# A router taken apart by row tile, fixed room for every expert in DRAM, and the experts' low parts on one engine

## The chip, the cores and the metric

The kernel runs on one core of a Trainium2 chip. The metric is the time of one execution on the device, in microseconds (us). Three timed runs of the kernel before gave 829.58, 831.20 and 831.58 us; their median, 831.2 us, is the time before.

## What is computed

One layer of a gated trunk over 512 rows of width 1024, all in float32:

```
xn = rms_norm(x, norm1_g)
x  = x + hybrid_mixer(xn, ...)        # attention, spatial gating and recurrence; gated, merged, then @ w_out
xn = rms_norm(x, norm2_g)
g_logits = xn @ wg + bg               # 4 groups
e_logits = xn @ we + be               # 16 experts, 4 in a group
# the best group; in it the two best experts by softmax; their two weights are normalised, times the group's probability
for e in range(16):
    h = silu(xn @ w_gate[e]) * (xn @ w_up[e])        # 1024 -> 512
    y = y + combine[:, e] * (h @ w_down[e])          # 512 -> 1024
return rms_norm(x + y, final_norm_g)
```

Each row goes to two of 16 experts, so each expert has 64 rows on average. The kernel brings an expert's rows together in a tile of 128 rows; an expert with more than 128 rows gets further tiles.

## The kernel before

**Products.** Every weight is split in two, `w_hi` (rounded to the format of the matrix engine) by ScalarE (`split_hi`, L354, and `split_hi_loop`, L361) and the rest `w_lo` by a subtraction (`split_lo`, L366, and `split_lo_loop`, L372). A product is three matmuls (`three`, L988 to L990). Weights come in blocks of 128x1024, from a ring of four buffers before the experts and 24 (EVEN and ODD, 12 each) in them; `w_hi` and `w_lo` have four places each. Before the experts GpSimd makes the low parts. In the experts `on_pool(r)` is true for the first four blocks of the first tile alone; VectorE makes the low parts of all others.

**Stages.** First come the projections of `x` (8 blocks), four pairs of heads and channels (5 blocks each), the gates with the branch products (36 blocks), and the output projection: 4 blocks for columns 0 to 511 (PSUM banks 4 to 7), then 4 for columns 512 to 1023, this half by row tile `t` (banks 0 to 3). Between the loads of one pair and the next SyncE queues a quarter of the stores that fill `slots`, the DRAM room for the experts' rows, with zeros (L452): 24 tiles of 512 KB in all.

**Router.** For each row tile of the second half: VectorE adds `x` (L1610), ScalarE squares (L882), GpSimd takes the power -1/2 (L607), VectorE makes `xn2` (L1616), TensorE turns it (`turn_xn2`, L1185), ScalarE copies it (L889), TensorE multiplies by the router's weights (`logits`, L1176). With the logits of all 512 rows VectorE picks group and experts (L1655 to L1680), TensorE counts the rows ahead of each row at its expert (L1217, L1220), and VectorE makes the one-hot matrix of tile 0 in `silu` (L1689), the place of every row in `slots` (L1695 to L1717), the table of tiles (L1719 to L1729) and the weights (L1733 to L1742). TensorE gathers tile 0 by 64 matmuls with `silu` (L1251); ScalarE and VectorE split it in `xT_hi` and `xT_lo` (L901, L1747). GpSimd scatters `xn2` to `slots` by eight indirect DMAs (L618); the other tiles are read back from there.

**Experts.** Tile `i` uses 12 blocks: gate and up of tile `i` and down of the tile before, so the program's `tile(i)` ends with the result of expert `i-1`, which ScalarE copies (`y_part`, L920) and stores to `slots` over its own rows (L922). Tiles 1 to 13 are unrolled in pairs, those from 14 on are in a loop whose count and experts are loaded to registers from `tile_table`. Here there are 16 tiles. Room `k` of `slots` is expert `k`'s for its first 128 rows; rooms from 16 on are for what is over. At the end GpSimd gathers for each row its first expert's result (L645) once all tiles but the last are stored (`before_last_stored`), and its second when the last is stored (`all_stored`); VectorE adds them (L1804, L1823) and normalises (L1811, L1816).

**Order.** Each engine's program is written out by hand and runs in order, with semaphores between engines. VectorE's `link` makes the next instruction wait for the one it wraps. SyncE issues all loads; its loads of tile 2 from the fourth block on wait for the scatter.

## Time and profile before

| | |
|---|---|
| median of three runs | 831.2 us |
| the profiled execution's own time | 831.56 us |
| span, first to last instruction | 829.8 us |
| TensorE busy, mean granted clock | 773.4 us (93%), 0.969 |
| VectorE, ScalarE, GpSimd busy | 486.0, 448.5, 213.8 us |
| chain that ended last | PE 80%, DVE 8%, ACT 6%, issue 2%, DMA 2%, POOL 1% |

```profile
PE   6999999999999999999999957999999999999950
DVE  6603657576633223023122275788989898998955
POOL 3654333232323444444425143000000000000013
PEclk9999999999999999999999959999999999999995
```

Each digit is a fortieth of the span, 20.7 us: the engine's busy share in tenths and, in the last row, TensorE's granted clock in tenths of full speed. The matmul engine is full but for the start, slices 24 and 25 (the router) and the end.

### The profile page before, as it was taken

The numbers are of one execution on the slowest core, as the hardware profiler recorded it, in microseconds if no ns is written. First come the engines' busy times: TensorE is split into PE (matmuls) and PEld (weight loads), VectorE is DVE, ScalarE is ACT, GpSimd is POOL, SyncE is SP. The second block draws the span as 40 slices with busy tenths as digits, with TensorE's granted clock in tenths as the row PEclk, the third lists the DMA queues.
The fourth block names the chain that finished last, engine by engine and source line by source line (L and its number), as shares of the span: only waits on it lengthen the run. The fifth ranks groups of instructions, "written<-read, shape, count | busy, mean of one in ns | idle before, by whom it ended". The sixth has DMA issues, their size and how long they took to land.

```text
span 829.8 us, 10565 instructions
## 1 busy us (share of the span) xinstructions
PE 773.4 (93%) x3639; PEld 635.7 (77%) x3639; DVE 486.0 (59%) x640; ACT 448.5 (54%) x572; POOL 213.8 (26%) x126
## 2 busy tenths in 40 slices
PE   6999999999999999999999957999999999999950
PEld 4887888888788888888888856887888888787840
DVE  6603657576633223023122275788989898998955
ACT  6245565565642323223222306688887888887832
POOL 3654333232323444444425143000000000000013
PEclk9999999999999999999999959999999999999995
DMA  8664561612122443323357349999999999957945
GB/s 300 183 243 162 179 227 53 228 53 76 51 77 70 148 138 102 102 89 89 101 176 285 109 182 350 399 398 403 388 409 397 410 407 402 401 226 274 334 152 203
DMA packets 126490, 186.24 MB, mean 224 GB/s; under 512 B 9133, under 2 KB 61941, under 8 KB 126454
## 3 DMA queue, kind: packets, MB, share of 16 engines
q1 hardware_dynamic: 119156, 167.82, 56.3%
q10 hardware_dynamic: 4994, 9.56, 3.0%
q0 software_dynamic: 2304, 8.39, 2.8%
q8 instruction: 22, 0.36, 0.2%
q14 instruction: 14, 0.11, 0.0%
HBM read 158.47 MB, written 27.28 MB: 224 GB/s over the span
## 4 chain that ended last, share of the span: by engine, by line
PE 80%; DVE 8%; ACT 6%; issue 2%; DMA 2%; POOL 1%; ACTq 1%; DVEq 0%; SPq 0%
PE ps L988 24%; PE ps L990 23%; PE ps L989 23%; PE ps L1228 2%; DVE w_lo L372 1%; PE ps L1251 1%; PE ps L1066 1%; PE ps L1092 1%; PE ps L1176 1%; ACT w_hi L361 1%; PE ps L1235 1%; DMA x<-in_x 1%; DMA slots<-y_tile 1%; DMA raw_mg<-slots,slot_idx 1%; PE ps L1077 1%
## 5 line engine op out<-in xcount | busy, mean ns | idle before, releaser
L366 POOL TENSOR_TENSOR w_lo<-raw,w_hi 128x1024 fp32r<-128x1024 f32 x72 | 174.0, 2419 | 256.5 <-ACT w_hi L354 256.5
L354 ACT ACTIVATE w_hi<-raw 128x1024 fp32r<-128x1024 f32 x73 | 77.0, 1058 | 182.5 <-PE ps L990 174.7
L988 PE MATMUL ps<-xn_hi,w_hi 128*128 128x512 f32 x352 | 141.8, 403 | 0.0
L990 PE MATMUL ps<-xn_hi,w_lo 128*128 128x512 f32 x352 | 137.2, 390 | 0.0
L989 PE MATMUL ps<-xn_lo,w_hi 128*128 128x512 f32 x352 | 137.0, 389 | 0.0
L988 PE MATMUL ps<-w_hi,xT_hi 128*128 128x512 f32 x256 | 104.1, 407 | 8.9 <-DVE xT_lo L1747 5.5
L990 PE MATMUL ps<-w_hi,xT_lo 128*128 128x512 f32 x256 | 101.3, 396 | 0.0
L989 PE MATMUL ps<-w_lo,xT_hi 128*128 128x512 f32 x256 | 101.1, 395 | 0.0
L645 POOL DMA_INDIRECT raw_mg<-slots,slot_idx x7 | 6.9, 986 | 300.4 <-ACTq L971 291.3
L989 PEld LDWEIGHTS ps<-xn_lo,w_hi 128*128 128x128 f32 x352 | 66.2, 188 | 15.1 <-issue 1.9
L988 PEld LDWEIGHTS ps<-xn_hi,w_hi 128*128 128x128 f32 x352 | 66.2, 188 | 14.8 <-issue 1.9
L990 PEld LDWEIGHTS ps<-xn_hi,w_lo 128*128 128x128 f32 x352 | 66.1, 188 | 14.1
L372 DVE TENSOR_TENSOR w_lo<-raw_mg,w_hi 128x1024 fp32r<-128x1024 f32 x57 | 67.9, 1221 | 3.7 <-ACT w_hi L361 1.7
L988 PEld LDWEIGHTS ps<-w_hi,xT_hi 128*128 128x128 f32 x256 | 48.8, 191 | 24.6 <-DVE w_lo L372 9.4
L361 ACT ACTIVATE w_hi<-raw_mg 128x1024 fp32r<-128x1024 f32 x57 | 59.7, 1058 | 10.6 <-PE ps L990 10.6
L1560 DVE SCALAR_TENSOR_TENSOR macc<-raw,ps 128x512 f32<-128x512 f32 x16 | 11.0, 687 | 92.7 <-PE ps L990 92.5
L372 DVE TENSOR_TENSOR w_lo<-raw,w_hi 128x1024 fp32r<-128x1024 f32 x43 | 51.3, 1221 | 13.5 <-ACT w_hi L361 13.5
L990 PEld LDWEIGHTS ps<-w_hi,xT_lo 128*128 128x128 f32 x256 | 48.9, 191 | 10.7
L989 PEld LDWEIGHTS ps<-w_lo,xT_hi 128*128 128x128 f32 x256 | 48.9, 191 | 9.4
L988 PE MATMUL ps<-w_hi,hT_hi 128*128 128x512 f32 x128 | 51.2, 400 | 2.9 <-DVE hT_lo L1754 2.9
L361 ACT ACTIVATE w_hi<-raw 128x1024 fp32r<-128x1024 f32 x43 | 43.9, 1054 | 15.9 <-PE ps L990 15.9
L990 PE MATMUL ps<-w_hi,hT_lo 128*128 128x512 f32 x128 | 49.9, 390 | 0.0
(282 smaller groups left out, 1438.6 us busy)
## 6 DMA issues: line engine op xcount, KB each, us to landing
raw<-in_w_in SPq DMA_DIRECT2D x52, 512.0 KB, 3.7
raw_mg<-in_exp_w_down SPq DMA_DIRECT2D x36, 512.0 KB, 8.0
...
```

What stands on the lines that cost most here:

```text
L354: nc.scalar.activation(w_hi[:, b % HI_SLOTS, :], raw_buf(b), ACT.Copy)\
L361: nc.scalar.activation(w_hi[:, (8 + r) % HI_SLOTS, :], buf, ACT.Copy).then_inc(S["hi_act"], 1)
L366: eng.tensor_tensor(w_lo[:, b % HI_SLOTS, :], raw_buf(b), w_hi[:, b % HI_SLOTS, :].bitcast(F32), ALU.subtract)\
L372: eng.tensor_tensor(w_lo[:, (8 + r) % HI_SLOTS, :], place(at, r)[0], w_hi[:, (8 + r) % HI_SLOTS, :].bitcast(F32), ALU.subtract)\
L988: pe.matmul(dst, hi_l, hi_r, start=start, stop=False)
L989: pe.matmul(dst, hi_l, lo_r, start=False, stop=False)
L990: return pe.matmul(dst, lo_l, hi_r, start=False, stop=stop)
L1066: mm = pe.matmul(ps[:, 4 + g % 2, at:at + w], qT[:, jp % 2, i * P:(i + 1) * P], keys_of(jp)[:, h, 0:w], start=True, stop=True)
L1077: mm = pe.transpose(ps[:, 6, kt * P:(kt + 1) * P], probs_of(g)[:, kt * P:(kt + 1) * P], ident[:, :])
L1092: mm = pe.matmul(ps[:, 7, i * P:(i + 1) * P], values_of(jp)[:, kt, 2 * h:2 * h + 2, :].rearrange("p q d -> p (q d)"), probsT[:, at + kt * ...
L1228: mm = pe.transpose(ps[:, 3 + k // 4, (k % 4) * P:(k % 4 + 1) * P], rows[:, k * P:(k + 1) * P], ident[:, :])
L1560: dve.scalar_tensor_tensor(out=macc[:, 1, :], in0=gate_buf[:, g % 3, :], scalar=1.0, in1=ps[:, 2 + c, :], op0=ALU.add, op1=ALU.mult)\
```

## The change

- **Slots.** Every expert has four tiles of room, its own 512 rows: `slots` grows from 24 to 65 tiles, all filled with zeros. A row's place is then its expert's start plus its count, which one matmul chain gives (`counts` starts from `start_bf`). Further tiles of an expert are found by `block_table`, from which ScalarE and SyncE load a register for each tile of the last loop.
- **Router.** `xn2` is split in half rows. `x + product` and its product with `norm2_g` (`x2_half`), the turn and the logits (`turn_half`, `half_logits`) are made for half a row tile at a time, unscaled; the row's factor is applied to the logits afterwards (`choose`) and by ScalarE to `xn2` (`x2_scale`). The dictionary `beside` names after which product of the output projection's second half each of them stands in TensorE's program. VectorE picks the experts by row tile (`choose`), then the counts, the one-hot matrix and the places by row tile (`send`), and GpSimd scatters by row tile. Tile 0 is gathered by `place0`, and split in two halves.
- **What is moved.** The table of further tiles (`overflow_table`) stands behind the low parts of the first tile; the two exponentials and the weights (`combine_weights`), and the order of the two gathers (`gather_order`), stand at the end of the experts.
- **Low parts.** `on_pool` is gone: VectorE makes all the experts' low parts, the first four among them.

The diff, cut; lines keep their sign and lose their first eight or twelve blanks. The old router's removal (L1590 to L1742) is not shown.

```diff
-SLOT_TILES = MAX_TILES + 1
...
+PER_EXPERT = TOK // P
+SLOT_TILES = NE * PER_EXPERT + 1
...
+def split_lo_loop(at, r):
+    nc.vector.wait_ge(S["hi_act"], loop_block(at.i, r) + 1)
+    nc.vector.tensor_tensor(w_lo[:, (8 + r) % HI_SLOTS, :], place(at, r)[0],
                       w_hi[:, (8 + r) % HI_SLOTS, :].bitcast(F32), ALU.subtract)\
-       .then_inc(S["lo_pool"] if on_pool(8 + r) else S["lo_dve"], 1)
+       .then_inc(S["lo_dve"], 1)
...
-load_tile(PAIRED, EVEN, 2, PAIRED, PAIRED - 1)
+load_tile(PAIRED, EVEN, 2, PAIRED, PAIRED - 1, (PAIRED + 1) * PER_EXPERT)
...
-    load_tile(n + (PAIRED - 1), EVEN, 1, e, before)
+    block = sp.value_load(block_table[0:1, bass.ds(n + (PAIRED + 1), 1)], min_val=0,
+                          max_val=SLOT_TILES - 1)
+    load_tile(n + (PAIRED - 1), EVEN, 1, e, before, block)
...
-for r in range(AHEAD):
-    split_lo(pool, B_EXP + r)
...
+def scatter(t):
+    if t == 0:
+        pool.wait_ge(S["zeros_stored"], 16 * SLOT_TILES)
+    pool.wait_ge(S["xn2_done"], t + 1)
+    pool.wait_ge(S["routed"], t + 1)
     for k in range(2):
         pool.indirect_dma_start(
             slots, bass.IndirectOffsetOnAxis(ap=slot_idx[:, 2 * t + k:2 * t + k + 1], axis=0),
             xn2[:, t, :], None).then_inc(S["scattered"], 16)
...
+x2_power(0)
+for t in range(1, NT):
+    x2_power(t)
+    scatter(t - 1)
+scatter(NT - 1)
...
+pool.wait_ge(S["routed"], NT + 1)
...
+def x2_square(half, t):
+    n = NT * half + t
+    act.wait_ge(S["x2_done"], n + 1)
+    if n > 0:
+        act.wait_ge(S["x2_sq"], n)
+    act.activation(y_tile[:, 0:512], x_rows[:, t, 512 * half:512 * (half + 1)], ACT.Square,
+                   accum_out=stat[:, 4 * half, t:t + 1]).then_inc(S["x2_sq"], 1)
+def take_turned(n):
+    act.wait_ge(S["turned_ps"], n + 1)
+    if n >= 4:
+        act.wait_ge(S["logits_ps"], n - 3)
+    act.activation(quarters[:, n % 4, :], ps[:, 4, :], ACT.Copy).then_inc(S["turned_done"], 1)
+def x2_scale(t):
+    act.wait_ge(S["x2_rstd"], t + 1)
+    act.activation(xn2[:, t, :], xn2[:, t, :], ACT.Copy, scale=stat[:, 5, t:t + 1])\
...
+for t in range(NT):
+    x2_square(0, t)
+    take_turned(t)
+for t in range(NT):
+    x2_square(1, t)
+    if t == NT - 2:
+        split_hi(B_EXP)
+    take_turned(NT + t)
+    x2_scale(t)
+    if t == NT - 2:
+        split_hi(B_EXP + 1)
+        split_hi(B_EXP + 2)
...
+split_hi(B_EXP + AHEAD)
+act.wait_ge(S["xT0_ps"], 1)
+act.activation(xT_hi[:, 0:4, :].rearrange("p k n -> p (k n)"), ps[:, 6, :], ACT.Copy)\
+   .then_inc(S["xT0_hi_done"], 1)
+act.wait_ge(S["xT_ps"], 1)
+act.activation(xT_hi[:, 4:8, :].rearrange("p k n -> p (k n)"), ps[:, 7, :], ACT.Copy)\
+   .then_inc(S["xT_hi_done"], 1)
+for r in range(1, 8):
...
-    y_part(loop_block(i, PER_TILE), at)
...
+    y_part(loop_block(i, PER_TILE), at, block)
...
+def block_of(tile_index):
+    return act.value_load(block_table[0:1, bass.ds(tile_index + 1, 1)], min_val=0,
+                          max_val=SLOT_TILES - 1)
...
-    tile(at_even(q))
-    tile(at_odd(q))
+    tile(at_even(q), (2 * q - 1) * PER_EXPERT)
+    tile(at_odd(q), 2 * q * PER_EXPERT)
...
-    tile(at_last(n))
+    tile(at_last(n), block_of(n + (PAIRED - 2)))
...
+act.wait_ge(S["exp_in"], 2)
+act.activation(route[:, 4, 0:4 * NG], route[:, 3, 0:4 * NG], ACT.Exp).then_inc(S["exp_done"], 1)
+act.activation(route[:, 12, :], route[:, 10, :], ACT.Exp).then_inc(S["exp_done"], 1)
+last_block = block_of(n_last + (PAIRED - 2))
...
+def turn_half(half, t):
+    n = NT * half + t
+    pe.wait_ge(S["x2g_done"], n + 1)
+    if n > 0:
+        pe.wait_ge(S["turned_done"], n)
+    for k in range(4):
+        mm = pe.transpose(ps[:, 4, k * P:(k + 1) * P],
+                          xn2[:, t, 512 * half + k * P:512 * half + (k + 1) * P], ident[:, :])
+    mm.then_inc(S["turned_ps"], 1)
...
+    pe.wait_ge(S["turned_done"], n + 1)
+    dst = ps[:, t, 32:32 + NG + NE] if half else ps[:, 5, t * 32:t * 32 + NG + NE]
+    for k in range(4):
+        mm = pe.matmul(dst, quarters[:, n % 4, k * P:(k + 1) * P], router_w[:, 4 * half + k, :],
+                       start=(k == 0), stop=(k == 3))
+    mm.then_inc(S["logits_ps"], 1)
...
+        pe.wait_ge(S["consts_pool"], 3)
+        pe.wait_ge(S["consts_dve"], 4)
+    pe.wait_ge(S["picked"], t + 1)
+    pe.matmul(ps[:, t, 0:NE], tri[0:2, 1, :], start_bf[:, :], start=True, stop=False)
+    for u in range(t + 1):
+        mm = pe.matmul(ps[:, t, 0:NE], tri[:, 0 if u == t else 1, :], picked_bf[:, u, :],
+                       start=False, stop=(u == t))
+    mm.then_inc(S["counts_ps"], 1)
...
+def totals():
...
+    mm.then_inc(S["counts_ps"], 1)
...
+def place0(t):
+    pe.wait_ge(S["tile0_where"], t + 1)
     pe.wait_ge(S["xn2_done"], t + 1)
...
+    for h in range(2):
+        for k in range(4):
+            mm = pe.matmul(ps[:, 6 + h, k * P:(k + 1) * P],
+                           xn2[:, t, (4 * h + k) * P:(4 * h + k + 1) * P], silu[:, t * P:(t + 1) * P],
+                           start=(t == 0 and k == 0), stop=(t == NT - 1 and k == 3))
+        if t == NT - 1:
+            mm.then_inc(S["xT_ps"] if h else S["xT0_ps"], 1)
...
+beside = {(0, 3): ((turn_half, 0, 0),), (0, 5): ((turn_half, 0, 1),), (0, 6): ((half_logits, 0, 0),),
+          (0, 7): ((turn_half, 0, 2),),
+          (1, 0): ((half_logits, 0, 1),), (1, 1): ((turn_half, 0, 3), (half_logits, 0, 2)),
+          (1, 3): ((half_logits, 0, 3),), (1, 4): ((turn_half, 1, 0),), (1, 6): ((half_logits, 1, 0),),
+          (2, 2): ((turn_half, 1, 1),), (2, 3): ((counts, 0),), (2, 4): ((half_logits, 1, 1),),
+          (3, 2): ((turn_half, 1, 2),), (3, 3): ((counts, 1),), (3, 4): ((half_logits, 1, 2),)}
...
+            for job, *which in beside.get((t, k), ()):
+                job(*which)
+counts(NT - 2)
+place0(0)
+turn_half(1, NT - 1)
+place0(1)
+half_logits(1, NT - 1)
+place0(2)
+counts(NT - 1)
+place0(NT - 1)
+totals()
...
-pe.wait_ge(S["tile0_where"], 1)
-for k in range(KD):
-    for t in range(NT):
-        mm = pe.matmul(ps[:, 3 + k // 4, (k % 4) * P:(k % 4 + 1) * P], xn2[:, t, k * P:(k + 1) * P],
-                       silu[:, t * P:(t + 1) * P], start=(t == 0), stop=(t == NT - 1))
-mm.then_inc(S["xT_ps"], 1)
-pe.wait_ge(S["xT_done"], 1)
 for r in range(8):
+    if r == 0:
+        pe.wait_ge(S["xT0_done"], 1)
+    if r == 2:
+        pe.wait_ge(S["xT_done"], 1)
...
+def x2_half(half, t):
+    at = slice(512 * half, 512 * (half + 1))
+    dve.tensor_tensor(x_rows[:, t, at], ps[:, t if half else 4 + t, :], x_rows[:, t, at], ALU.add)\
+       .then_inc(S["x2_done"], 1)
+    if half == 0 and t == 0:
+        dve.wait_ge(S["g2_in"], 16)
+    dve.wait_ge(S["x2_done"], NT * half + t + 1)
+    dve.tensor_tensor(xn2[:, t, at], x_rows[:, t, at], g2_rows[:, at], ALU.mult)\
+       .then_inc(S["x2g_done"], 1)
...
+def x2_mean(t):
+    dve.wait_ge(S["x2_sq"], NT + t + 1)
+    dve.scalar_tensor_tensor(out=stat[:, 4, t:t + 1], in0=stat[:, 4, t:t + 1], scalar=1.0 / D,
+                             in1=stat[:, 0, t:t + 1], op0=ALU.mult, op1=ALU.add)\
+       .then_inc(S["x2_stat"], 1)
...
+def choose(t):
...
+    dve.wait_ge(S["logits_ps"], NT + t + 1)
+    link(dve.tensor_tensor(lg, ps[:, t, 32:32 + NG + NE], early[:, 32 * t:32 * t + NG + NE], ALU.add))
+    dve.wait_ge(S["x2_rstd"], t + 1)
+    link(dve.scalar_tensor_tensor(out=lg, in0=lg, scalar=stat[:, 5, t:t + 1], in1=router_b[:, :],
+                                  op0=ALU.mult, op1=ALU.add))
+    link(dve.tensor_reduce(g_max[:, t:t + 1], lg[:, 0:NG], AX.X, ALU.max))
+    link(dve.tensor_scalar(a, lg[:, 0:NG], g_max[:, t:t + 1], -2 * NEG, ALU.is_equal, ALU.mult))
+    link(dve.tensor_tensor_scan(out=b, data0=a, data1=zeros16[:, 0:NG], initial=0.0,
+                                op0=ALU.add, op1=ALU.add))
+    link(dve.scalar_tensor_tensor(out=c, in0=b, scalar=-2 * NEG, in1=a, op0=ALU.is_equal, op1=ALU.mult))
+    link(dve.scalar_tensor_tensor(out=em.rearrange("p (g e) -> p g e", g=NG), in0=spread(c, NG, EPG),
+                                  scalar=NEG, in1=lg[:, NG:].rearrange("p (g e) -> p g e", g=NG),
+                                  op0=ALU.add, op1=ALU.min))
+    link(dve.max(m, em))
+    dve.tensor_tensor(first[:, 0:1], m[:, 0:1], m[:, 1:2], ALU.is_gt)
+    link(dve.tensor_scalar(row(17, NE), em, m[:, 1:2], None, ALU.is_equal))
+    link(dve.tensor_tensor_scan(out=rank, data0=row(17, NE), data1=zeros16, initial=first[:, 0:1],
+                                op0=ALU.add, op1=ALU.add))
+    link(dve.scalar_tensor_tensor(out=rank, in0=rank, scalar=2.0, in1=row(17, NE),
+                                  op0=ALU.is_le, op1=ALU.mult))
+    dve.scalar_tensor_tensor(out=picked_bf[:, t, :], in0=em, scalar=m[:, 1:2], in1=rank,
+                             op0=ALU.is_gt, op1=ALU.add).then_inc(S["picked"], 1)
+    link(dve.scalar_tensor_tensor(out=chosen[:, t, :], in0=em, scalar=m[:, 1:2], in1=rank,
+                                  op0=ALU.is_gt, op1=ALU.add))
+    link(dve.tensor_scalar(four(1)[:, t:t + 1], chosen[:, t, 0:1], -far, far, ALU.mult, ALU.add))
+def send(t):
+    dve.wait_ge(S["counts_ps"], t + 1)
+    dve.scalar_tensor_tensor(out=silu[:, t * P:(t + 1) * P], in0=hid[:, 0:P],
+                             scalar=four(1)[:, t:t + 1], in1=ps[:, t, 0:1].to_broadcast([P, P]),
+                             op0=ALU.subtract, op1=ALU.is_equal).then_inc(S["tile0_where"], 1)
+    link(dve.tensor_tensor(where[:, t, :], ps[:, t, 0:NE], chosen[:, t, :], ALU.mult))
+    link(dve.max(top_slot[:, t, :], where[:, t, :]))
+    dve.tensor_scalar(slot_idx[:, 2 * t:2 * t + 2], top_slot[:, t, 0:2], -1.0, None, ALU.add)\
+       .then_inc(S["routed"], 1)
...
+def overflow_table():
+    dve.wait_ge(S["counts_ps"], NT + 1)
...
+    link(dve.tensor_tensor(over, spread(ps[:, 2, 2 * NE:3 * NE], NE, PER_EXPERT - 1),
+                           row(20, NE, PER_EXPERT - 1), ALU.is_gt))
+    link(dve.tensor_reduce(four(2)[:, 0:1], over.rearrange(flat), AX.X, ALU.add))
+    dve.tensor_scalar(tile_table[:, 0:1], four(2)[:, 0:1], float(NE - PAIRED + 1), None, ALU.add)
+    for n, (table, full) in enumerate(((block_table, NE * PER_EXPERT), (tile_table, NE))):
+        link(dve.tensor_tensor(weight, over, row(21 + n, NE, PER_EXPERT - 1), ALU.mult))
+        link(dve.max(eight[:, 8 * n:8 * n + 8], weight.rearrange(flat)))
+        dve.tensor_scalar(table[:, NE + 1:NE + 9], eight[:, 8 * n:8 * n + 8], -1.0,
+                          float(full), ALU.mult, ALU.add)
...
+                          ALU.mult, ALU.add)
+    dve.tensor_copy(block_table[:, 1:NE + 1], row(24, NE))
+    dve.tensor_copy(tile_table[:, 1:NE + 1], row(23, NE)).then_inc(S["tab"], 1)
+def gather_order():
...
+    dve.wait_ge(S["scattered"], 16 * 2 * NT)
+    link(dve.tensor_scalar(swap, at_first, last_rows[:, 0:1], None, ALU.is_ge))
+    link(dve.scalar_tensor_tensor(out=swap, in0=at_first, scalar=last_rows[:, 1:2], in1=swap,
+                                  op0=ALU.is_le, op1=ALU.mult))
...
+    dve.tensor_tensor(gathered[0], at_first, apart, ALU.add)
+    link(dve.tensor_tensor(gathered[1], at_second, apart, ALU.subtract))
+    idx = slot_idx[:, :].rearrange("p (t k) -> p t k", k=2)
+    for k in range(2):
+        last = dve.tensor_scalar(idx[:, :, k], gathered[k], -1.0, None, ALU.add)
+    last.then_inc(S["routed"], 1)
+def combine_weights():
+    for n, (x, best, c, at) in enumerate(((logs[:, :, 0:NG], g_max, NG, 3),
+                                          (masked, top[:, :, 0], NE, 10))):
+        dve.tensor_tensor(row(at, NT, c), x, spread(best, NT, c), ALU.subtract)\
+           .then_inc(S["exp_in"], 1)
...
+dve.memset(start_bf[:, :], 1.0).then_inc(S["consts_dve"], 1)
+dve.wait_ge(S["consts_dve"], 3)
+dve.wait_ge(S["consts_pool"], 11)
+dve.tensor_copy(start_bf[0:1, :], route[0:1, 19, 0:NE]).then_inc(S["consts_dve"], 1)
+for t in range(NT):
+    x2_half(0, t)
+dve.wait_ge(S["x2_sq"], NT)
+link(dve.tensor_scalar(stat[:, 0, :], stat[:, 0, :], 1.0 / D, EPS, ALU.mult, ALU.add))
+for t in range(NT):
+    if t < NT - 1:
+        dve.wait_ge(S["x2_ps"], t + 1)
+    else:
+        dve.wait_ge(S["w_used"], B_EXP)
+    x2_half(1, t)
+    x2_mean(t)
+    if t == 0:
+        dve.wait_ge(S["logits_ps"], NT)
+        link(dve.tensor_copy(early, ps[:, 5, 0:NT * 32]))
+    if t > 0:
+        send(t - 1)
+    if t == NT - 2:
+        split_lo(dve, B_EXP)
+    choose(t)
+send(NT - 1)
...
+dve.wait_ge(S["xT0_hi_done"], 1)
+dve.tensor_tensor(xT_lo[:, 0:4, :].rearrange("p k n -> p (k n)"), ps[:, 6, :],
+                  xT_hi[:, 0:4, :].rearrange("p k n -> p (k n)").bitcast(F32), ALU.subtract)\
+   .then_inc(S["xT0_done"], 1)
+split_lo(dve, B_EXP + 1)
+dve.wait_ge(S["xT_hi_done"], 1)
+dve.tensor_tensor(xT_lo[:, 4:8, :].rearrange("p k n -> p (k n)"), ps[:, 7, :],
+                  xT_hi[:, 4:8, :].rearrange("p k n -> p (k n)").bitcast(F32), ALU.subtract)\
+   .then_inc(S["xT_done"], 1)
+for r in range(2, 8):
+    split_lo(dve, B_EXP + r)
+for r in range(AHEAD):
+    split_lo_loop(at_odd(0), r)
+overflow_table()
...
+split_lo_loop(at_last(n_last), AHEAD)
+gather_order()
+combine_weights()
```

## Rows read from the trace of the kernel before

**Rows 1.** A window each: us, busy by engine (count), granted clock, DMA share, GB/s

```profile
53.00:59.00 6.00, 6.00 (x28) 4.97 (x27) 0.16 (x2) 2.88 (x6) 2.96 (x2) 1.00 1.03 418
350.00:400.00 50.00, 50.00 (x222) 41.44 (x221) 10.88 (x12) 14.26 (x17) 21.78 (x9) 1.00 0.32 96
475.00:495.00 20.00, 11.24 (x65) 11.03 (x65) 12.74 (x54) 3.59 (x6) 7.86 (x4) 0.50 0.52 182
502.00:507.00 5.00, 4.88 (x14) 3.88 (x15) 1.01 (x2) 1.23 (x2) 4.21 (x3) 0.66 0.93 375
518.00:526.00 8.00, 7.22 (x25) 5.74 (x26) 4.36 (x5) 3.18 (x3) 0.00 (x0) 0.79 1.04 386
```

**Rows 2.** The chain of waits, 470 to 520 us: start, duration, engine, what, line

```profile
481.12 2.21 DVE route L1641
...
489.31 10.38 PE ps L1251 x64
```

**Rows 3.** Timeline of TensorE: start, duration, line, what, count, idle before it

```profile
460.79 1.86 PE L1176 MATMUL ps<-router_w,xn2T 128*128 128x20 f32 x16
...
502.12 0.61 PE L988 MATMUL ps<-w_hi,xT_hi 128*128 128x512 f32 x1 [2.44 <-DVE xT_lo L1747]
...
514.74 1.04 PE L1228 MATMUL ps<-ident,xn 128*128 128x128 f32 x8
518.78 0.50 PE L988 MATMUL ps<-w_hi,xT_hi 128*128 128x512 f32 x1 [3.01 <-DVE xT_lo L1747]
```

**Rows 4.** Timeline of VectorE, 443 to 518 us

```profile
443.85 2.48 DVE L1602 TENSOR_TENSOR x_rows<-ps,x_rows 128x512 f32<-128x512 f32 x4 [16.15 <-PE ps L990]
...
485.66 0.23 DVE L1676 SCALAR_TENSOR_TENSOR route<-route 128x64 f32<-128x64 f32 x1
485.92 0.22 DVE L1677 TENSOR_REDUCE route<-route 128x4 f32<-128x64 f32 x1
...
492.91 0.17 DVE L1716 CAST slot_idx<-route 128x4 int32<-128x4 f32 x1
492.99 0.16 DVE L1717 CAST slot_idx<-route 128x4 int32<-128x4 f32 x1
...
513.50 3.50 DVE L372 TENSOR_TENSOR w_lo<-raw,w_hi 128x1024 fp32r<-128x1024 f32 x3 [1.63 <-ACT w_hi L361]
```

**Rows 5.** Timeline of GpSimd, 448 to 484 us

```profile
448.54 0.23 POOL L603 IOTA hid<- 128x128 f32 x1
...
476.31 6.98 POOL L366 TENSOR_TENSOR w_lo<-raw_a,w_hi 128x1024 fp32r<-128x1024 f32 x3 [4.55 <-ACT w_hi L354]
```

**Rows 6.** Timeline of ScalarE: pairs, first tile, ends of two tiles

```profile
72.31 1.06 ACT L354 ACTIVATE w_hi<-raw 128x1024 fp32r<-128x1024 f32 x1 [3.90 <-PE ps L990]
...
77.75 1.06 ACT L354 ACTIVATE w_hi<-raw 128x1024 fp32r<-128x1024 f32 x1 [3.29 <-PE ps L990]
...
510.63 1.28 ACT L907 ACT_TABLE_LOAD   x1
...
576.63 2.01 ACT L361 ACTIVATE w_hi<-raw_c 128x1024 fp32r<-128x1024 f32 x2 [1.10 <-PE ps L990]
...
759.03 2.00 ACT L361 ACTIVATE w_hi<-raw_c 128x1024 fp32r<-128x1024 f32 x2 [1.70 <-PE ps L990]
```

**Rows 7.** Timeline of VectorE at the end

```profile
797.06 1.23 DVE L372 TENSOR_TENSOR w_lo<-raw_c,w_hi 128x1024 fp32r<-128x1024 f32 x1 [0.25 <-ACT w_hi L361]
...
814.83 1.28 DVE L1823 SCALAR_TENSOR_TENSOR raw_mg<-raw_mg,w_first 128x1024 f32<-128x1024 f32 x1 [4.65 <-DMA raw_mg<-slots,slot_idx]
```

**Rows 8.** Timeline of GpSimd at the end

```profile
797.87 1.27 POOL L645 DMA_INDIRECT raw_mg<-slots,slot_idx  x1 [291.35 <-ACTq L971]
...
810.46 0.94 POOL L645 DMA_INDIRECT raw_mg<-slots,slot_idx  x1 [7.58 <-ACTq L974]
```

**Rows 9.** Timeline of SyncE's queue, 48 to 60 us

```profile
49.09 6.12 SPq L452 DMA_DIRECT2D slots<-raw  x6
55.25 4.70 SPq L400 DMA_DIRECT2D raw<-in_w_in  x2
```

More of the change, by code:

```diff
@@ L941, in _, with tile @@
             xT_hi_part(2)
-            def tile(at):
+            def tile(at, block):
                 i = at.i
@@ new lines, in _ @@
+            masked, top, chosen, where, top_slot = (row(n, NT, c) for n, c in ((7, NE), (8, 8), (9, NE), (11, NE), (13, 8)))
+            gathered, last_rows = (four(8), four(9)), four(10)
+            zeros16, early = row(18, NE), row(5, NT * 32)
+            far = float(2 * SLOT_TILES * P)
+            def x2_half(half, t):
[7 more added lines that the diff above has]
+                   .then_inc(S["x2g_done"], 1)
```

325 lines of the change are left out of this document (78 added, 247 removed).

## Prediction

> **What bounds the kernel now.** I read the page's 40 slices first: TensorE is full but for the start, slices 24 and 25 and the end. The windows then give the two prices of a product. In the steady stretch 222 matmuls fill 50 us, so one of 128x512 takes 0.225 us and the three of a step 0.68; where the granted clock is 0.50 (the level of 1.2 GHz) one takes nearly double [rows 1]. The chain of waits between 470 and 520 us shows the hole: VectorE's routing and 10.4 us of gathering tile 0 by matmul [rows 2]. TensorE's timeline has the first expert product at 502.12 and tile 1's first at 518.78, 16.7 us later, both released by VectorE's `xT_lo` [rows 3]. The second half of the output projection begins at 443.8 (VectorE is released at 443.85 [rows 4]). So the stretch that the change rewrites is 58.3 us, of which the products themselves are 96 x 0.227 = 21.8 us.
>
> **The router, worked out as one chain.** Times are those of the trace of before.
>
> 1. *Start.* VectorE now waits for all of GpSimd's constants before its first half row. GpSimd ends them at 448.77; two more iotas of the size of the others make it 449.0 [rows 5]. VectorE then copies, adds and multiplies (0.2, 0.69, 0.69; the four adds of before took 2.48 [rows 4]): the first half row is ready at 450.7. TensorE wants it after 12 products, at 446.5. It stands 4.2 us, and with it everything behind.
> 2. *To the first full logits.* 15 steps of three products (10.2), five turns of four (eight took 1.04 with the overlap, so 0.44) and five logits of four (16 took 1.86, so 0.43) [rows 3]: 443.8 + 4.2 + 14.6 = 462.6.
> 3. *One row tile.* `choose` has 12 linked small operations up to `picked` and one unlinked. Linked ones of 64 elements start 0.26 apart, those of 16 last 0.05 less, an unlinked one costs 0.08 (two casts start 0.08 apart) [rows 4]: 12 x 0.22 + 0.08 = 2.7 us, then 0.4 for two more, 1.4 for the next half row. TensorE: turn 0.44, two steps of products 1.36, counts 0.3, logits 0.43. That is 6.6 us, with ten semaphores at 0.04 between engines 7.0 a row tile, against 5.44 + 1.17 = 6.6 for TensorE's own work: VectorE's chain becomes the bound here. Two rounds: 476.6. GpSimd's power and ScalarE's half squares and copies lie beside the products.
> 4. *The end.* The low part of block 0 comes before `choose(2)` (to 477.6), which ends at 480.3; half row at 482.1, turn, `place0(1)`, logits: 484.9. The 64 matmuls of before took 10.38 us, eight of them 1.3 [rows 2]; at a low clock throughout eight take 1.8, which I use. `choose(3)` 487.6, counts and one-hot 488.4, `place0(3)` 1.8, half split 0.58 and 0.68 with the first half overlapped: first expert product at 490.7 instead of 502.1. **Gain 11.4 us.** The top-8 operation `max` is not in the trace; it is taken as a linked one of 0.21. From below it can't be under the 0.08 of an unlinked one, from above I take the 2.21 us that one small operation took [rows 2]; GpSimd was then at three low parts [rows 5], of which it has none left here, so the value of the other small ones is nearer. One `max` a row tile is on the chain: -0.5 to +8 us for four, taken at 0.
>
> **The clock.** After the 3.0 us stop before tile 1 the granted clock was 0.79 in the mean of 8 us [rows 1, 3]: 3.3 us at half, 1.65 lost. After the 2.44 us stop before tile 0 it was lower still. The stop of 4.2 us in point 1 gets one such fall, the 1.8 us stop in row tile 2 (465.3 to 467.1: the turn waits for VectorE), shorter than either, half of one. **Loss 2.5 us** (0 to 6.6). The Trainium skill ("TensorE: Matmul & The Clock Gate", "A second HAM failure mode: psum-queue depth-cycling") says that an engine that idles briefly between groups of matmuls often enough swings between the two levels and pays for it each time. By that rule all four stops of the new order (4.2, 1.8, 0.5, 1.6 us) would cost one fall each; it is a rival below.
>
> **Tile 0 and the way to tile 1.** VectorE now makes ten low parts here (blocks 1 to 10) instead of seven, at 1.2 us each [rows 4]. Seven of them fit under TensorE's 1.36 us a block; the delay of the last is 0.5. Behind it comes `overflow_table`: 11 linked operations at 0.22 to 0.26 and 8 unlinked at 0.08, 3.1 us, in front of `hid` and `xT_lo`, which TensorE waits for. Nothing covers it: `xT_lo` was last there already. **Loss 3.6 us**, bounds 2 and 5. TensorE's stop grows from 3.0 to 6.2 us; the fall after it is there before and after.
>
> **Steady tiles 1 to 13.** No operation is added; block addresses are register arithmetic. 0.
>
> **The last tiles.** At tile 13's end ScalarE loads a register; the first `w_hi` after the result's copy came 1.70 us after the last instruction instead of 1.10 [rows 6], and tile 14 began that much later. `block_of` puts such a load at the head of two tiles, where ScalarE is behind. **Loss 1.2 us** (0 if the sequencer hides it, 2).
>
> **The tail.** `gather_order` (8 small operations, 1.3 us) stands behind the last low part, which ends at 798.3 [rows 7]; then two exponentials with a table load of 1.28 us as before the first silu [rows 6], about 0.5, and a register load, all ahead of `before_last_stored`. The first gathers start at about 802.5 instead of 797.87 and overlap the last store. The second gathers start at 810.46 and the first sum on them at 814.83 [rows 7, 8]; the sums on the first gathers, 11 us after their start in the trace (ending at 810.2), then end at about 814. **Loss 0.8 us** (0 to 3).
>
> **The zeros.** 41 more stores of 512 KB. In the window with nothing else they go at 418 GB/s [rows 1], 1.25 us each; SyncE issued six in 6.12 us and the next load behind them [rows 9]. With 16 that first load (block 13) moves at 72 and lands at 74.5; ScalarE wanted it at 72.31 and the next at 77.75 [rows 6]. ScalarE is 2 us late once, under a block of TensorE's (5.4 us). Loss 0, bounds 0 and 2 for the forecast. The skill ("DMA: Bandwidth & Descriptors", "Queues, rings and completion order") says that each engine takes a queue's descriptors in ring order, so the load can't pass the zeros; without that order block 13 would be in time and the cost 0 as well. The other three pairs have longer covers.
>
> **The sum.** -11.4 + 2.5 + 3.6 + 1.2 + 0.8 = -3.3 us on the profiled execution's 831.56: 828.3. The median is 0.36 lower: **828.0 us**. With the terms' middles moved to their nearer bounds this case covers 825 to 831.
>
> **Rivals.**
> - *A: the stops cost less than I think.* VectorE's constants are not late for the chain (another bound ends later), `overflow_table` runs in half its time, no fall of the clock. Then 4 to 7 us of the losses go: about 822.5. For it: the rows of single small operations are all there is of VectorE's new chain. Against: GpSimd's constants follow its last low part, whose time is fixed by TensorE. Chance 0.15.
> - *B: the clock swings through the whole router.* Four falls instead of one and a half, 1.65 each, +4.1, and `place0` and tile 0's first blocks at half for longer, +1: 833, no change. For it: the trace has a clock at 0.50 from 475 to 495 even though TensorE was busy for 11.2 of 20 us [rows 1]. Against: 24 products stand between most stops. Chance 0.2.
> - *C: slower, the zeros.* The loads behind 16 zeros come too late. It decides at a store of 1.43 us: then block 13 lands after 77.5, ScalarE's copies for TensorE's next block are late, and each pair is held. At 1.9 us a store, half as much again as in the window, the burst ends 7.5 us past that cover in the two pairs where ScalarE has least room: +14, less what the chain of the pair had in hand, 3: +11, 839. For it: the stores share the engines with the column loads. Against: 418 GB/s in the window. Chance 0.12.
>
> **How the numbers follow.** Forecast case 0.53, A 0.15, B 0.20, C 0.12. A difference of 0.3%, 2.5 us, is about what a measurement of this kernel can tell from none: below 828.7 is faster, above 833.7 slower. Of the forecast case two thirds lie below 828.7 (0.35) and the rest between (0.18). Faster 0.15 + 0.35 = 0.50; same 0.18 + 0.14 of B = 0.32; slower 0.06 of B and 0.12 of C = 0.18. The range takes half of A and all of B: 823 to 834.5.
>
> **What would show it.** In the changed trace: TensorE idle for about 4 us at 446.5 to 450.7, released by VectorE's `xn2`; row tiles 7 us apart in `picked_bf`; the first expert product near 490.7 plus the falls (492 to 494); TensorE idle for 6 us before tile 1, released by `xT_lo`, with `route` and the tables just ahead on VectorE; tiles 14 and 15 each 0.6 us longer; the first gather after 802 relative to the end of before. The forecast is wrong if the first expert product comes after 497, if the pairs (100 to 220 us) take longer at all, or if the steady tiles' 18.2 us change.

## The result, and the profile after

The changed kernel takes 833.8 us (median of 9 runs, 833.2 to 839.7); the kernel before took 830.9 beside it. The ratio is 1.0046 [1.0025, 1.0067]: slower by 0.5%, where 828.0 and "faster" had been forecast. The profiled execution took 833.76 us (span 831.9, mean granted clock 0.977) against 831.56 (829.8, 0.969).

Three rows of the page of the kernel after, a fortieth of the span (20.8 us) a digit:

```profile
PE   7999999999999999999997987999999999998950
POOL 3654333232323444444425130000000000000013
PEclk9999999999999999999999998999999999999985
```

Slice 21 (437 to 458 us) has fallen from full to 7, slice 23 (478 to 499) has filled from 5 to 8 and its clock risen from 5, and slice 24 is 7 as before (slices counted from 0). A hole was moved forward and shrank less than forecast. Where both kernels pass the same points (after less before, in us):

| point | forecast | measured | step, measured |
|---|---|---|---|
| first expert product | -8.9 | 498.70 - 502.12 = -3.4 | router, with its clock |
| tile 1's first product | -5.3 | 516.89 - 518.78 = -1.9 | +1.5 |
| tile 2's turns | -5.3 | 529.83 - 531.90 = -2.1 | -0.2 |
| turns at tile 13's end | -5.3 | 747.88 - 749.77 = -1.9 | +0.2 |
| last turns of rows | -4.1 | 786.92 - 787.15 = -0.2 | +1.7 |
| copy of the last result | -4.1 | 803.96 - 802.71 = +1.2 | +1.5 |
| end of the span | -3.3 | 831.9 - 829.8 = +2.1 | +0.9 |

TensorE in the router of the kernel after (start, duration, line, what, count, idle before it and who ended it), which answers to [rows 3]:

```profile
451.82 1.12 PE L1172 MATMUL ps<-ident,xn 128*128 128x128 f32 x4 [5.11 <-DVE xn L1653]
...
466.82 0.96 PE L1184 MATMUL ps<-router_w,xn2T 128*128 128x20 f32 x8
...
472.57 0.66 PE L1172 MATMUL ps<-ident,xn 128*128 128x128 f32 x4 [1.97 <-DVE xn L1653]
...
480.48 0.66 PE L1172 MATMUL ps<-ident,xn 128*128 128x128 f32 x4 [0.52 <-DVE xn L1653]
...
487.26 2.03 PE L1210 MATMUL ps<-silu,xn 128*128 128x128 f32 x16
489.13 0.60 PE L1172 MATMUL ps<-ident,xn 128*128 128x128 f32 x4
...
495.25 0.18 PE L1193 MATMUL ps<-start_bf,tri 2*128 2x16 bf16 x1 [1.06 <-DVE picked_bf L1686]
...
498.70 0.50 PE L983 MATMUL ps<-w_hi,xT_hi 128*128 128x512 f32 x1 [0.43 <-DVE xT_lo L1810]
...
512.01 1.09 PE L1252 MATMUL ps<-ident,xn 128*128 128x128 f32 x8 [1.95 <-DMA xn<-slots]
516.89 0.79 PE L983 MATMUL ps<-w_hi,xT_hi 128*128 128x512 f32 x1 [3.78 <-DVE xT_lo L1792]
```

The stops are where they were forecast, with the releasers that were forecast; the row L1184 holds a surprise: a half row's logits are four products in the code and eight in the record, 0.81 us from start to start. VectorE of the same kernel, against [rows 4]:

```profile
450.22 0.16 DVE L1767 CAST start_bf<-route 1x16 bf16<-1x16 f32 x1 [5.88 <-POOL hid L591]
...
469.44 0.18 DVE L1679 MAX8 route<-route 128x8 f32<-128x16 f32 x1
...
470.49 0.23 DVE L1686 SCALAR_TENSOR_TENSOR picked_bf<-route 128x16 bf16<-128x16 f32 x1
...
512.09 0.20 DVE L1707 TENSOR_TENSOR route<-ps,route 128x48 f32<-128x48 f32 x1
...
515.02 0.68 DVE L1807 TENSOR_TENSOR hid<-silu,ps 128x512 f32<-128x512 f32 x1
515.62 1.22 DVE L1792 TENSOR_TENSOR xT_lo<-ps,xT_hi 128x1024 fp32r<-128x1024 f32 x1
```

It waits 5.88 us for GpSimd's last constant, chooses in 2.8 us (the top-8 operation 0.21, as taken), and `overflow_table` holds `hid` from 512.09 to 515.02. Windows of the kernel after (us, busy by engine and count, granted clock, DMA share, GB/s), against [rows 1]:

```profile
452.00:456.00 4.00, 4.00 (x16) 3.33 (x17) 3.65 (x6) 1.33 (x4) 0.00 (x0) 0.61 0.01 2
476.00:498.00 22.00, 18.68 (x133) 16.05 (x132) 14.68 (x64) 9.10 (x13) 8.11 (x9) 1.00 0.67 234
516.00:520.00 4.00, 3.11 (x7) 2.48 (x8) 1.97 (x2) 0.09 (x1) 0.00 (x0) 0.50 1.03 380
798.00:800.00 2.00, 2.00 (x6) 1.52 (x6) 1.43 (x11) 0.45 (x3) 0.00 (x0) 0.53 0.00 0
```

The clock is at its lower level (1.2 GHz) after the first stop, after tile 1's, and, new, in the last block, but at the higher level (2.4 GHz) from 476 to 498. Last, ScalarE at the heads of tiles 14 and 15 and GpSimd, against [rows 6, 5, 8]:

```profile
758.19 3.90 ACT L345 ACTIVATE w_hi<-raw_c 128x1024 fp32r<-128x1024 f32 x4 [2.75 <-issue]
...
777.13 3.90 ACT L345 ACTIVATE w_hi<-raw_c 128x1024 fp32r<-128x1024 f32 x4 [1.60 <-issue]
```

```profile
448.19 1.73 POOL L587 IOTA route<- 128x16 f32 x7
...
801.21 0.98 POOL L615 DMA_INDIRECT raw_mg<-slots,slot_idx  x1 [300.61 <-ACTq L966]
...
812.84 0.94 POOL L615 DMA_INDIRECT raw_mg<-slots,slot_idx  x1 [6.91 <-ACTq L969]
```

The row of seven iotas is named after its first; taken by shape (count, busy us, mean ns of one) they are

```profile
L587 POOL IOTA route<- 128x48 f32 x4 | 1.6, 442 | 0.0
L587 POOL IOTA route<- 128x16 f32 x3 | 0.5, 197 | 0.0
```

### The profile page after: what moved, and what is told of

It is laid out like the page before. It is cut to its first block, busy times and chain, and to the rows that moved or that the text cites. A ratio compares the mean times of both kernels' runs of the same rounds, so it can differ in the third digit from the quotient of the medians.

```text
span 831.9 us, 10721 instructions
## 1 busy us (share of the span) xinstructions
PE 772.2 (93%) x3643; PEld 631.3 (76%) x3643; DVE 496.9 (60%) x707; ACT 455.2 (55%) x591; POOL 206.8 (25%) x124
## 4 chain that ended last, share of the span: by engine, by line
PE 77%; DVE 9%; ACT 6%; issue 3%; DMA 2%; POOL 1%; ACTq 1%; DVEq 0%; SPq 0%
PE ps L983 23%; PE ps L985 23%; PE ps L984 23%; DVE w_lo L356 2%; PE ps L1252 2%; PE ps L1061 1%; PE ps L1087 1%; ACT w_hi L345 1%; DMA slots<-y_tile 1%; ACT xn L901 1%; PE ps L1259 1%; DMA x<-in_x 1%; ACT w_hi L338 1%; PE ps L1184 1%; DMA raw_mg<-slots,slot_idx 1%
## 5 line engine op out<-in xcount | busy, mean ns | idle before, releaser
L345 ACT ACTIVATE w_hi<-raw 128x1024 fp32r<-128x1024 f32 x43 | 43.9, 1054 | 17.2 <-PE ps L985 17.2
L984 PE MATMUL ps<-w_lo,hT_hi 128*128 128x512 f32 x128 | 50.4, 394 | 0.0
```

The lines of the kernel that those rows point to most:

```text
L345: nc.scalar.activation(w_hi[:, (8 + r) % HI_SLOTS, :], buf, ACT.Copy).then_inc(S["hi_act"], 1)
L984: pe.matmul(dst, hi_l, lo_r, start=False, stop=False)
```

## The experiments

Ratios are to the kernel before, run beside each; spans are of one profile each.

| kernel | median us | ratio, 95% interval | span |
|---|---|---|---|
| changed | 833.8 | 1.0046 [1.0025, 1.0067] | 831.9 |
| constants later | 830.4 | 0.9992 [0.9969, 1.0015] | 828.0 |
| table later | 833.5 | 1.0026 [1.0010, 1.0043] | 833.4 |
| tail reordered | 834.3 | 1.0037 [1.0017, 1.0057] | 829.6 |
| register load later | 835.3 | 1.0051 [1.0035, 1.0067] | 832.8 |
| all edits | 825.7 | 0.9923 [0.9897, 0.9950] | 823.9 |
| all edits, stops filled | 822.0 | 0.9883 [0.9855, 0.9911] | 820.2 |
| logits twice | 843.2 | 1.0145 [1.0115, 1.0175] | 840.6 |
| before, more zeros | 830.6 | 0.9989 [0.9967, 1.0011] | 826.9 |
| changed, stops filled | 830.3 | 0.9999 [0.9980, 1.0018] | 828.4 |
| before, stops filled | 828.8 | 0.9980 [0.9961, 0.9999] | 826.4 |

**Constants later.**

```diff
-dve.wait_ge(S["consts_pool"], 11)
-dve.tensor_copy(start_bf[0:1, :], route[0:1, 19, 0:NE]).then_inc(S["consts_dve"], 1)
 for t in range(NT):
     x2_half(0, t)
+dve.wait_ge(S["consts_pool"], 11)
+dve.tensor_copy(start_bf[0:1, :], route[0:1, 19, 0:NE]).then_inc(S["consts_dve"], 1)
```

> The changed kernel with VectorE's wait for GpSimd's constants (and the copy behind it) moved from ahead of the four first half rows to behind them. Theory W (the stop at the start of the router is this wait and nothing else): TensorE no longer stops for 5.1 us at 446.7, and the fall of the clock behind the stop (about 1.3 us in the changed kernel's trace) goes too. First expert product near 492.3 instead of 498.7, end of the span 6.4 us earlier, about 825.5 us. Theory M (another thing holds the first half row about as long: the second norm's gain row, a bank, GpSimd's last low part): the stop moves to the next wait and less than 2 us is gained. Theory D (the DMA stream of the experts' weights, share 1.05 from 500 to 740, is the real pace): the first expert product comes 6.4 us earlier, but the tiles stretch and the end gains under 2 us.

TensorE and a window of this kernel:

```profile
465.69 0.66 PE L1172 MATMUL ps<-ident,xn 128*128 128x128 f32 x4 [1.97 <-DVE xn L1653]
...
491.81 0.50 PE L983 MATMUL ps<-w_hi,xT_hi 128*128 128x512 f32 x1 [0.43 <-DVE xT_lo L1810]
...
510.03 0.80 PE L983 MATMUL ps<-w_hi,xT_hi 128*128 128x512 f32 x1 [4.35 <-DVE xT_lo L1792]
...
755.08 0.80 PE L983 MATMUL ps<-w_hi,xT_hi 128*128 128x512 f32 x1 [2.05 <-DVE w_lo L356]
```

```profile
512.00:516.00 4.00, 4.00 (x11) 3.14 (x10) 1.22 (x1) 1.44 (x2) 0.00 (x0) 0.50 1.02 371
```

Theory W holds at the router: no stop, first expert product 6.9 us earlier, tile 1's too. But the end came 3.9 earlier in the profile and 3.4 in the medians, not 6.4. Between tile 1's first product and tile 2's turns it took 14.4 us instead of 12.9: the fall behind the stop was longer here. And behind tile 14's stop, 2.05 us here and 2.10 in the changed kernel, the clock fell here and not there. The tiles between kept their pace (542.41 to 742.43: 200.02 us; in the changed kernel 547.85 to 747.88: 200.03), so theory D is out.

**Table later.** All of `overflow_table` but its first operation moves into tile 1.

```diff
-overflow_table()
+overflow_table(0)            # the comparison that reads the counts
 hidden(B_EXP + 8, 1)
 xT_lo_part(2)
...
     split_lo_loop(at, r + AHEAD)
+    if first and r == 0:
+        overflow_table(1)    # the rest
```

> The changed kernel with all of the overflow table but its first operation moved behind hid, xT_lo and one low part of tile 1, where VectorE waits 3.0 us for ScalarE. Theory T (the table stands in front of what TensorE waits for): xT_lo starts when ScalarE's xT_hi is done, near 514.0 instead of 515.6, tile 1's first product 1.6 us earlier, end 1.6 us earlier. Rival: the load of tile 1's rows (the turns waited 1.95 us for it) and ScalarE's copies set that start, and the gain is under 0.5 us; or the clock falls all the same and the gain is given back in the next 8 us.

```profile
501.74 0.50 PE L983 MATMUL ps<-w_hi,xT_hi 128*128 128x512 f32 x1 [0.43 <-DVE xT_lo L1812]
...
518.19 0.50 PE L983 MATMUL ps<-w_hi,xT_hi 128*128 128x512 f32 x1 [2.37 <-DVE xT_lo L1794]
```

From tile 0's first product to tile 1's it is 16.45 us instead of 18.19, 1.7 less, and 1.5 of it is there at the end (331.7 us from the first expert product, against 333.2). The whole span was longer only because this execution reached tile 0 3.0 us later: 1.5 before the stop at 474, 1.6 behind it, where the clock fell here. In the medians the gain is not told from nothing.

**Tail reordered.** On VectorE `gather_order` and the two subtractions go ahead of the last low part; on ScalarE the exponentials go behind `before_last_stored`.

```diff
-split_lo_loop(at_last(n_last), AHEAD)
 gather_order()
-combine_weights()
+combine_weights(lambda: split_lo_loop(at_last(n_last), AHEAD))
...
 act.sem_inc(S["before_last_stored"], 1)
+act.wait_ge(S["exp_in"], 2)
+act.activation(route[:, 4, 0:4 * NG], route[:, 3, 0:4 * NG], ACT.Exp).then_inc(S["exp_done"], 1)
+act.activation(route[:, 12, :], route[:, 10, :], ACT.Exp).then_inc(S["exp_done"], 1)
```

> The changed kernel with the tail reordered: the order of the gathers and the two subtractions ahead of the last low part on VectorE, the two exponentials behind the release of the first gathers on ScalarE. Theory G (the last store took 1.1 us longer, from its issue to the second gathers 7.7 us instead of 6.5, because the first gathers started late and lie beside it): first gathers near 798 instead of 801.2, second gathers 1.1 us earlier, end 0.8 to 1.1 us earlier. Rival: the store takes 7.7 us all the same and the end doesn't move (within 0.3 us).

```profile
798.12 1.90 POOL L615 DMA_INDIRECT raw_mg<-slots,slot_idx  x1 [297.53 <-DVE slot_idx L1741]
...
810.50 0.94 POOL L615 DMA_INDIRECT raw_mg<-slots,slot_idx  x1 [6.74 <-ACTq L969]
```

The last result's copy stands where it stood (803.89), the second gathers start 2.3 us earlier, and the end comes 2.3 us earlier: twice what theory G gave. That this is the edit's doing is not shown. From that copy to the second gathers it took 6.6 us here and 8.9 in the changed kernel; it took 7.9 with constants later and 7.5 with the changed kernel's stops filled, both without this edit, and 8.7 and 8.8 with all edits, which have it. From the copy to the end it is 25.7 us here, 27.4 to 27.9 in the six profiles of the changed kernel's own tail, and 28.5 and 28.6 with all edits. The first gathers did start 3 us sooner; what sets the time of the last store is open, and the median (834.3) shows no gain.

**Register load later.** `block_of` for tiles 14 and 15 is called at the ninth block of the tile instead of at its head.

```diff
-    tile(at_last(n), block_of(n + (PAIRED - 2)))
+    tile(at_last(n), None, n + (PAIRED - 2))
...
+        if r == 8 and tile_index is not None:
+            block = block_of(tile_index)
```

> The changed kernel with ScalarE's load of the block number moved from the head of the two last full tiles to their ninth block, where ScalarE waits for TensorE. Theory R (two register loads in a row hold ScalarE at the head of tile 14, one at the head of tile 15): TensorE's stops before these tiles go from 2.10 to 1.03 and from 0.94 to 0.32 us, and the end comes 1.7 us earlier. Rival: the load has to drain ScalarE wherever it stands, costs the same 0.5 to 1 us at the ninth block and TensorE stops there: under 0.5 us gained.

```profile
763.54 0.50 PE L985 MATMUL ps<-w_hi,xT_hi 128*128 128x512 f32 x1 [1.08 <-DVE w_lo L356]
...
781.91 0.50 PE L985 MATMUL ps<-w_hi,xT_hi 128*128 128x512 f32 x1 [0.34 <-DVE w_lo L356]
```

The two stops are back at the kernel before's 1.03 and 0.32: theory R. Between turns at 751.86 and 789.35 it takes 37.5 us instead of 39.0. The median did not improve: in this profile the clock fell behind the stop at 474 (a turn of 1.04 us) and longer in tile 1.

**Logits twice.**

```diff
-for k in range(4):
+for k in 2 * list(range(4)):
     mm = pe.matmul(dst, quarters[:, n % 4, k * P:(k + 1) * P], router_w[:, 4 * half + k, :],
```

> The changed kernel with each half row's four logits products issued twice, the second time over the first, so that the result is the same. In the trace four of them took 0.81 us, not the 0.43 of the prediction. Theory L (they stand in the chain of every row tile): the first full logits come 5 x 0.81 = 4.1 us later, each of the three row tiles behind 0.81 more, first expert product 6.5 us later, near 505.2, end the same 6.5 us later. By the size that the prediction gave them it would be 3.4. Rival V (behind the first full logits VectorE's chain is the bound and TensorE has room): only the first 4.1 us.

```profile
477.00 0.66 PE L1172 MATMUL ps<-ident,xn 128*128 128x128 f32 x4 [1.92 <-DVE xn L1653]
...
502.02 0.18 PE L1193 MATMUL ps<-start_bf,tri 2*128 2x16 bf16 x1 [1.20 <-DVE picked_bf L1686]
```

The turn behind the first full logits comes 4.4 us later (it was at 472.57), the last counts 6.8 later (495.25): five times 0.89 and eight times 0.85. Theory L, at the size of the record or a little over it; rival V is out. Tile 1 starts 7.6 later, the end 8.7 (medians 9.4); the excess over 6.8 comes where the clock is low, in row tile 3's gather (3.65 us instead of 2.05) among others.

**Before, more zeros.** In the kernel before `SLOT_TILES = 65` instead of 24.

> The kernel before with 65 blocks of zeros stored instead of 24, and nothing else. Theory N (the stores are hidden): the pairs keep their pace, the time is that of the kernel before within 0.3%. Theory C (the loads behind a burst of 16 stores come too late for TensorE): the pairs between 72 and 220 us stretch, 3 to 11 us.

```profile
797.00:800.00 3.00, 3.00 (x9) 2.33 (x8) 0.00 (x0) 0.00 (x0) 2.39 (x3) 0.50 0.42 117
```

No change in the median. Theory C is out: the output projection's second half begins 0.5 us behind the kernel before's, and 0.3 us behind it in the changed kernel. The window shows something else. In this kernel, whose last block is that of the kernel before, the clock fell behind the stop ahead of that block, as it did in the changed kernel, and it did not fall behind the stops ahead of tiles 0 and 1 (3.01 us again), where the profile of the kernel before has two falls.

**All edits.** The four edits above and

```diff
+place0(0)
 counts(NT - 2)
-place0(0)
 turn_half(1, NT - 1)
-place0(1)
+place0(1, (0,))
 half_logits(1, NT - 1)
+place0(1, (1,))
 place0(2)
```

> All four edits tried one by one (wait for the constants behind the first half rows, rest of the overflow table in tile 1, tail reordered, block number loaded at the ninth block), and tile 0's products reordered: row tile 0's ahead of the counts of row tile 2, row tile 1's halves on both sides of the last half logits. Theory S (the pieces add up): from the changed kernel's 831.9 span 6.9 for the start, 1.1 for the order of the products, 1.6 for the table, 1.7 for the register loads, 2.3 for the tail: span 818 to 819, ratio to the kernel before 0.987. Theory K (what is saved in TensorE's stops is partly given back by falls of its clock, as with the constants, where 6.9 us at the first expert product had become 3.9 at the end): one or two falls of 1.5 us more, span 820 to 823, ratio 0.99.

From the turn of row tile 2 to the first expert product it takes 17.1 us instead of 18.2: the order of the products gives 1.1. The span is 823.9, a little past theory K's range: the clock fell behind the 1.97 us stop at 467 (0.57 from 467 to 471), where it had not in the changed kernel, and behind tile 1's (0.55 from 508 to 512 us). At 825.7 us it is 0.8% faster than before.

**All edits, stops filled.** Products that nobody reads, in TensorE's stops.

```diff
+def keep_busy(n):
+    for _ in range(n):
+        pe.matmul(ps[:, 7, 0:P], ident[:, :], ident[:, :], start=True, stop=True)
...
+(2, 2): ((keep_busy, 5), (turn_half, 1, 1)),
...
 turn_x(x_odd, S["x_odd_in"], 16)
+keep_busy(7)
...
 turn_h(tiles)
+keep_busy(9)
 pe.wait_ge(S["hT_done"], tiles)
```

> The kernel with all edits, and products of the identity with itself into a bank that nobody reads where TensorE waits: five ahead of the turns of row tile 1's second half, seven behind the turns of tile 1's rows, nine behind the last turns of hid, about 0.24 us each. They leave shorter stops (about 0.8, 0.8 and 0.7 us). Theory K (falls of the clock behind stops of 2 to 4 us are part of the price): the products behind these three places run at 2.4 GHz (0.23 us apart) in every profile, and the end comes 1.5 to 4 us before that of the kernel with all edits. Rival: the falls come from the whole stretch and not from those stops, or the fillers delay the turns: the same or up to 1 us slower.

TensorE and a window:

```profile
464.34 1.27 PE L1192 MATMUL ps<-ident 128*128 128x128 f32 x10
466.47 0.66 PE L1174 MATMUL ps<-ident,xn 128*128 128x128 f32 x4 [0.85 <-DVE xn L1662]
...
509.02 0.50 PE L985 MATMUL ps<-w_hi,xT_hi 128*128 128x512 f32 x1 [0.81 <-DVE xT_lo L1804]
...
785.87 0.49 PE L985 MATMUL ps<-w_hi,hT_hi 128*128 128x512 f32 x1 [0.84 <-DVE hT_lo L1811]
```

```profile
508.00:512.00 4.00, 3.19 (x15) 2.50 (x15) 3.79 (x14) 1.71 (x2) 0.00 (x0) 1.00 1.05 413
```

Theory K: 3.7 us less in span and median, and the five runs lie within 1.2 us (820.9 to 822.1) where the kernel without fillers has 822.9 to 826.4. It is the fastest kernel here, 1.2% before the kernel before.

**The two kernels of the comparison, stops filled.** The changed one has 18, 5, 11 and 9 such products in its four long stops, the one before 4, 28, 7, 9 and 9 in its five; nothing is moved.

> The changed kernel, nothing moved, with products of the identity with itself (0.24 us each, into a bank that nobody reads) in TensorE's stops: 18 ahead of the first turns, 5 ahead of the turns of row tile 1's second half, 11 ahead of tile 1's products, 9 ahead of the last block's. Theory K: the changed kernel's trace had falls of the clock behind three of these stops (1.3, 1.6 and 1.3 us); all go, span 827.7, median 829.5, and the spread of its runs (833.2 to 839.7) shrinks to about 1 us. By the rival, that the clock has no part in what was lost, the time stays at 833.8.

> The kernel before with the same products in its stops: 4 ahead of the last turns, 28 behind the last logits, 7 ahead of tile 0's products, 9 ahead of tile 1's and 9 ahead of the last block's. Theory K: tile 0's 64 products take 7.6 us instead of 10.4 and tile 0's and tile 1's first blocks run at 2.4 GHz: 2.8 + 0.6 + 1.6 = 5 us less, span 825, median 826. With both kernels free of falls the changed one is then 3 us slower on its own: the clock has not made the difference between them. Rival: the kernel before gains less than 4.2 us, so that with even clocks the change would be worth nothing or a gain.

Changed, and then before:

```profile
446.63 4.18 PE L1190 MATMUL ps<-ident 128*128 128x128 f32 x36
451.91 0.66 PE L1172 MATMUL ps<-ident,xn 128*128 128x128 f32 x4 [1.10 <-DVE xn L1659]
...
515.41 0.50 PE L983 MATMUL ps<-w_hi,xT_hi 128*128 128x512 f32 x1 [1.69 <-DVE xT_lo L1798]
```

```profile
759.00:763.00 4.00, 4.00 (x14) 3.33 (x13) 2.95 (x3) 1.98 (x3) 0.00 (x0) 0.58 1.05 407
```

```profile
487.94 0.41 PE L1223 MATMUL ps<-picked_bf,tri 128*128 128x16 bf16 x10 [3.27 <-DVE picked_bf L1689]
...
489.49 9.04 PE L1257 MATMUL ps<-silu,xn 128*128 128x128 f32 x64 [1.05 <-DVE silu L1698]
```

The changed kernel gains 3.5 us in span and median, but its runs still spread over 3.5 us (828.5 to 832.0) and not over the 1 expected, and its profile still has one fall: at tile 14, behind a stop of 1.88 us that was not filled (the window above; turns to turns that tile took 21.5 us, and 20.1 in the changed kernel, where no fall followed 2.10 us). The one before gains 3.4 in its span and about 1.7 by its ratio, less than the 5 expected: behind 3.27 us that stayed unfilled, the 64 records still began at the lower level, and took 9.0 us where 7.6 had been expected. So neither is free of falls; each has one left, of about 1.4 us. As they are, the changed kernel is slower by 2.0 us in span and 1.4 in median (the twelve runs of each give 0.5 to 2.2, at 95%, for the difference of the means). So with most of the falls gone the change still brings no gain; by these medians about half of the 2.9 us between the two is the clock, by the spans hardly any of it.

## Why the prediction was wrong, step by step

- **Start (point 1): right in place and releaser, 1.1 us short.** The stop was 5.1 us, not 4.2. "Two more iotas of the size of the others" failed: in the kernel before five took 0.61 us (the three of 128x16 0.14 each in mean, one of 128x64 0.19), here seven took 1.73, four of them of 128x48 at 0.44 each. Size alone does not explain that price; its cause is open.
- **To the first full logits (point 2): the mis-sized term.** Forecast 11.9 us behind the stop, measured 16.0. "16 took 1.86, so 0.43" counted records as instructions: an fp32 product stands in the trace as two, so [rows 3]'s 16 are the eight products of a row tile, and a half row's four cost about half of 1.86: 0.81 us from start to start in the kernel after. Five times 0.4 is 2.0 us here, and three times more behind it: 3 us in all. The doubled logits showed both the size and that all eight are on the chain. Another 1.5 of the 4.1 was the fall of the clock, priced apart; most of the rest is the return to the products (a step of three takes 0.78 us behind a small job, 0.68 elsewhere, and there are ten such jobs up to here).
- **Row tiles (point 3): the bound was right, the pitch not.** `picked_bf` comes 7.9, 8.4 and 8.2 us apart; the working has 7.0, 8.0 (with block 0's low part, 1.0) and 7.3. In the first, 0.4 of the 0.9 is the logits, and 0.4 is a slip of addition: the terms as given (2.7, 0.4 and 1.4; 0.44, 1.36, 0.3 and 0.43) make 7.0 before the semaphores, not 6.6, and 7.4 with them. Over the two rounds of point 3 the slip is 0.8 us. In the second, both come again, but the low part held the chain by only 0.3 us, not 1.0 (it ran from 482.88, while TensorE made the logits, and `choose(2)` began at 484.01). VectorE's own chain was right (2.8 for 2.7).
- **The end (point 4): about 1 us short behind block 0's low part.** 0.4 is the logits again; row tile 0's gather held the last turn by 0.3. A row tile's gather takes 1.8 to 1.9 us. The forecast had 1.8, by two errors that cancel: half the records, and the lower clock where it was the higher.
- **Sum of the router:** first expert product forecast at 490.7 + 2.5 of clock = 493.2, measured 498.7. These 5.5 us are the whole of the error; the other steps nearly cancel (forecast 5.6, measured 5.5).
- **Clock in the router: 2.5 forecast, about 1.5 taken.** It fell behind the 5.1 us stop and not behind the 1.97 us one, nor behind the three later ones of 0.5 to 1.2 us. Rival B did not happen in this profile. The Trainium skill ("TensorE: Matmul & The Clock Gate", "A second HAM failure mode: psum-queue depth-cycling") says that short idle periods, repeated, make the clock swing; the runs agree in kind only: with the same stop of 1.9 to 2.0 us the clock fell with table later, register load later and all edits, and not in the changed kernel or with constants later, tail reordered or logits twice.
- **Tile 0 to tile 1: 3.6 forecast, 1.5 measured.** `overflow_table` cost 2.9 (3.1), but the ten low parts were ready 1.4 us sooner behind the first product (13.4 us against 14.8), not 0.5 later. In the kernel before the first of tile 0's low parts were GpSimd's, and the clock in its first blocks was low.
- **Zeros and steady tiles: 0, right** (zeros shown by two kernels; 0.2 us over 13 tiles).
- **Last tiles: 1.2 forecast, 1.7 measured.** ScalarE waits 2.75 us at the first head, where the load stands behind that of `n_last`, and 1.60 at the second. Right, and shown by moving it.
- **Last block: not in the forecast, +1.5.** The stop ahead of it is 2.85 us in both kernels. The clock fell behind it here and not in the kernel before. That is no effect of the change: it fell in the kernel before with more zeros too, and did not fall with register load later and with all edits, which have the changed kernel's last block.
- **Tail: 0.8 forecast, 0.9 measured, and not shown.** The size fits, the mechanism doesn't: the sums on the first gathers were not last, the last store was (8.9 us from copy to second gathers, against 7.8), and with the tail reordered that time was 6.6 once and 8.7 and 8.8 twice. From copy to end the changed kernel's tail took 27.4 to 27.9 us in six profiles, the kernel before's 27.1, 26.2 and 23.9 in three: longer each time, but the kernel before's alone varies by more than the term.

The failed step is the price of a half row's logits in points 2 to 4, eight links of a chain at 0.43 us each, which measured 0.81: 3.0 us. With it the same working gives 831.0, no change instead of faster. The addition in point 3 put right makes it 831.8, and the 1.1 us of the start 832.9, against 833.8 measured; what else was missed nearly cancels (more: the last block's fall 1.5, the last tiles 0.5, returns to the products and small waits in the router about 2; less: the way to tile 1 2.1, the clock in the router 1.0, block 0's low part 0.7). That 832.9 comes so near to the measured 833.8 is in part luck, since falls of the clock that differ from profile to profile are among these parts.
